# Moving DRAM-to-DRAM copies of an expert table between the stages of a transformer kernel

## What is computed

```python
for i in range(2):                                   # two layers
    kv = mem_n @ mem_w_kv[i]
    x = x + 0.5 * swiglu(rmsnorm(x, norm_g[i, 0]), ffn_w_up[i, 0], ffn_w_down[i, 0])
    x = x + (pool_layer, diff_layer)[i](rmsnorm(x, norm_g[i, 1]), ...)
    x = x + 0.5 * swiglu(rmsnorm(x, norm_g[i, 2]), ffn_w_up[i, 1], ffn_w_down[i, 1])
...
x = x + g1 * hybrid_mixer(h, w_in, w_out, rel_bias)  # the last attention
# experts: 8 heads pick 16 of 16384 each, per token
s = einsum('bthpd,hpnd->bthpn', q, sub_keys); ...; e_idx = ...; g = softmax(g_s)
u = u_emb[e_idx]                                     # rows of U, 16384 x 1024
act = gelu(einsum('btd,bthkd->bthk', h, u))
out = einsum('bthk,bthkd->btd', g * act, v_emb[e_idx])   # rows of V, 16384 x 1024
```

## Time and profile before

| | |
|---|---|
| median of 3 runs | 2007.17 us (2002.93 to 2011.62) |
| profiled execution | 2008.95 us, span 2007.4 us |
| mean granted clock of TensorE | 0.952 |
| PE, DVE, ACT, POOL busy | 1774.0, 1277.5, 795.6, 652.1 us |
| DMA: SP's queue q1 | 346.15 MB, 50.4% of 16 engines' span |
| DMA: POOL's queue q0 | 301.52 MB, 37.6% |

### The profile page before, as it was taken

One profiled execution on the slowest core, in us unless ns is written; L12 is line 12 of the kernel. 1 busy time (PEld: TensorE's weight loads), 2 busy tenths in 40 slices (PEclk: granted clock), 3 DMA queues, 4 the chain that ended last, 5 costly groups with the idle time before them and its releaser, 6 DMA issues.

```text
span 2007.4 us, 22993 instructions
## 1 busy us (share of the span) xinstructions
PE 1774.0 (88%) x8110; PEld 1306.8 (65%) x8110; DVE 1277.5 (64%) x2212; ACT 795.6 (40%) x1423; POOL 652.1 (32%) x602
## 2 busy tenths in 40 slices
PE   7999999999999999999999789788688877778776
PEld 6887898887888779978777788675333333333332
DVE  4566766655466546766655577478999885555554
ACT  5444435544354436665443356432323322211111
POOL 4443560234015440111445112023334433333330
PEclk9999999999999999999999799889889989899998
DMA  8999976799899989758998656368999999999995
GB/s 268 326 373 381 305 257 252 261 348 373 290 313 347 373 282 337 259 206 306 330 335 300 201 193 204 105 256 328 420 420 420 420 420 419 420 421 421 421 421 224
DMA packets 247274, 649.99 MB, mean 324 GB/s; under 512 B 14945, under 2 KB 156562, under 8 KB 214418
## 3 DMA queue, kind: packets, MB, share of 16 engines
q1 hardware_dynamic: 200210, 346.15, 50.4%
q0 software_dynamic: 46304, 301.52, 37.6%
q10 hardware_dynamic: 672, 1.18, 0.3%
HBM read 643.56 MB, written 139.48 MB: 390 GB/s over the span
## 4 chain that ended last, share of the span: by engine, by line
PE 39%; DMA 28%; DVE 16%; POOL 8%; ACT 4%; issue 4%; SPq 0%; ACTq 0%; DVEq 0%; POOLq 0%
DMA late_uv<-uv_rows,M 12%; DMA adaW<-in_w_ada 10%; PE P L1254 6%; PE P L717 3%; PE P L718 3%; PE P L719 3%; PE PX L800 3%; DVE WL L1773 3%; DMA early_uv<-uv_rows,M 3%; PE PX L802 3%; PE PX L801 3%; POOL adaW L554 2%; POOL adaW L555 2%; DVE early_uv L2357 2%; PE P L666 2%
## 5 line engine op out<-in xcount | busy, mean ns | idle before, releaser
L1773 DVE TENSOR_TENSOR WL<-WR,WH 128x1024 fp32r<-128x1024 f32 (+1 forms) x246 | 323.5, 1356 | 213.3 <-ACT WH L1300 213.0
L1300 ACT ACTIVATE WH<-WR 128x1024 fp32r<-128x1024 f32 (+1 forms) x272 | 270.7, 1044 | 357.1 <-PE P L719 154.0
L1254 PE MATMUL P<-early_uv,M 128*128 128x512 f32 x544 | 260.4, 635 | 56.2 <-ACT M L1711 56.2
L1254 PE MATMUL P<-late_uv,M 128*128 128x512 f32 x480 | 240.8, 660 | 78.0 <-ACT M L1711 78.0
L800 PE MATMUL PX<-WH,hTh 128*128 128x512 f32 x704 | 280.8, 399 | 7.6 <-DVE WL L1781 4.3
L802 PE MATMUL PX<-WH,hTl 128*128 128x512 f32 x704 | 275.9, 392 | 0.0
L801 PE MATMUL PX<-WL,hTh 128*128 128x512 f32 x704 | 275.0, 391 | 0.0
L1788 DVE TENSOR_TENSOR WL<-WR,WH 128x1024 fp32r<-128x1024 f32 x128 | 185.1, 1486 | 135.8 <-ACT WH L1309 135.7
L1254 PEld LDWEIGHTS P<-late_uv,M 128*128 128x128 f32 x480 | 99.4, 213 | 218.2 <-issue 117.7
L1254 PEld LDWEIGHTS P<-early_uv,M 128*128 128x128 f32 x544 | 108.0, 203 | 204.5 <-issue 133.6
L651 POOL DMA_INDIRECT early_uv<-uv_rows,M x136 | 130.1, 956 | 286.2 <-PE P L1254 182.9
(11 more groups left out here) (365 smaller groups left out, 3175.7 us busy)
## 6 DMA issues: line engine op xcount, KB each, us to landing
WR<-in_ffn_w_up SPq DMA_DIRECT2D x88, 1024.0 KB, 9.9
WR<-in_ffn_w_down SPq DMA_DIRECT2D x44, 1024.0 KB, 11.1
uv_rows<-in_peer_u SPq DMA_DIRECT2D x35, 1024.0 KB, 13.5
uv_rows<-in_peer_v SPq DMA_DIRECT2D x35, 1024.0 KB, 14.9
uv_rows<-in_peer_u SPq DMA_DIRECT2D x58, 512.0 KB, 9.6
uv_rows<-in_peer_v SPq DMA_DIRECT2D x58, 512.0 KB, 9.1
adaW<-in_w_ada POOLq DMA_DIRECT2D x48, 512.0 KB, 8.1
WR<-in_diff_w_in SPq DMA_DIRECT2D x14, 1024.0 KB, 11.6
```

Of the source, the lines that this page charges most:

```text
L1254: last = mm(P[2 * t + q][:], diag[:, n % 2, i], rows_uv(n)[:, i, D + q * 512:D + q * 512 + 512], start=n % GROUPS == 0 and i == 0, stop=n ...
L1300: nc.scalar.activation(split_view(WH, U % 2, kind, part), raw(c % 2, kind, h, part), copy)\
L1773: tt(split_view(WL, U % 2, kind, part), raw(c % 2, kind, h, part), split_view(WH, U % 2, kind, part).bitcast(F32), ALU.subtract)\
```

## The change

Only the tables of the copies change, and one condition around the copy in the loop, since a count may now be 0 there. `COPIES` and `IN_LOOP` are in units. In sum, before and after: kv 4 and 8 units; pool_in to pool_out 7 and 16; diff_in 14 and 28; diff_out 3 and 6; in2 7 and 28; out2 0 and 2; the four down stages 36 and 24; the written-out chunks of the up stages 9 and 0; the loops 48 and 16. A copy is now of up to 512 rows, where it was of up to 256. The number of copies (pairs of DMAs) falls from 93 to 69.

```diff
-    COPIES = dict(kv0=(1, 1), kv1=(1, 1), pool_in=(1, 1, 1), group=(1,), pool_outx=(1,), pool_out=(1, 1), diff_in=(2,) * 7,
-                  diff_out=(1, 1, 1), in2=(1,) * 7, up00=(0, 0, 0), up01=(1, 1, 1), up10=(1, 1, 1), up11=(1, 1, 1),
-                  down00=(2, 1) * 3, down01=(2, 1) * 3, down10=(2, 1) * 3, down11=(2, 1) * 3)
-    IN_LOOP = (1, 2)
+    COPIES = dict(kv0=(2, 2), kv1=(2, 2), pool_in=(3, 3, 3), group=(2,), pool_outx=(1,), pool_out=(2, 2), diff_in=(4,) * 7,
+                  diff_out=(2, 2, 2), in2=(4,) * 7, out2=(2, 0), up00=(0, 0, 0), up01=(0, 0, 0), up10=(0, 0, 0), up11=(0, 0, 0),
+                  down00=(1,) * 6, down01=(1,) * 6, down10=(1,) * 6, down11=(1,) * 6)
+    IN_LOOP = (0, 1)
...
-            copies += 4 * len(IN_LOOP)
+            copies += 4 * sum(n > 0 for n in IN_LOOP)
...
-                    copy_rows(r * (128 * sum(IN_LOOP)) + (loop_from + 128 * sum(IN_LOOP[:j])), 128 * IN_LOOP[j])
+                    if IN_LOOP[j]:
+                        copy_rows(r * (128 * sum(IN_LOOP)) + (loop_from + 128 * sum(IN_LOOP[:j])), 128 * IN_LOOP[j])
```

## The result

The changed kernel takes 2037.3 us (median of three executions, 2033.7 to 2044.8) against 2005.7 for the kernel before, measured beside it. A fourth execution took 2255.6 us at a mean granted clock of 0.744, a slower state, and is left out. The ratio is 1.0161, with an interval of 1.0131 to 1.0192, so it is about 32 us slower. Measured once more (e11) it took 2041.1 us, with a ratio of 1.0197 (1.0148 to 1.0245). The forecast was 2033, range 1992 to 2087.

What follows compares the result with a forecast made beforehand. The prediction took PE as the bound, held up by DMA transfers as full in the feed-forward layers; 52 us of attention delays less 26 us gained is +26 us, forecast 2033 us, range 1992 to 2087.

Steps and rivals of the forecast that it cites:

- (a): Feed-forward layers: removing 53 of 93 copy units shortens PE's waits and restores its clock, a gain of 26 us.
- upper bound of 31.3 us: Feed-forward layers: the most that could be gained, 24.6 us of PE's waits plus 6.7 us of lost clock.
- adaW step: Feed-forward layers: PE's four waits for the sums of adaW vanish as POOL's transfers speed up, 10.6 us gained.
- (b): Attention stages: added copies make weights land late in SP's queue, delays of 9 + 30 + 13 = 52 us.
- queue sums: Attention stages: copies and weights between two splits take 87.3 us (kv and pool), 139.2 (differential) and 139.2 (last attention).
- cushion: Attention stages: each delay is reduced once by some 3 us lying between a weight split and PE's need of it.
- 3.5 us a unit: Copies of four units: average price, the first two units at 3.0 us, the last two halfway between 3.0 and 4.9.
- (c): SP's issues, POOL's first gather and the expert stage: moved or unchanged at no cost, the gather shifting with the delay.
- 1: Large copies stay slow at 4.9 us a unit, total 2136 us; halfway, at 4.2, 2087; chance 0.15.
- rival 2: Large copies cost 3.0 us a unit: 23 us late against 26 gained, net -3, 2004 us; chance 0.25.
- 3: Units cost 2.6 us as in a short burst, so the attention delays are small: net -20, 1987 us; chance 0.15.
- Rival 4: Expert stage: the last copy ends after 1320 us and sets the start of the gathers; given no chance of its own.

Runs made afterwards that it cites:

- e11: The changed kernel measured once more, unaltered, on another chip against the kernel before; 2041.1 us, ratio 1.0197.
- e1: Against the kernel before: the change's lighter copies in the feed-forward layers only, attention stages as before, 53 units left out; 1978.8 us, ratio 0.9877.
- e8: Against the kernel before: only the up stages' copies lightened as in the change, down and attention stages as before, 41 units left out; 1979.3 us.
- e5: Against the changed kernel: all 128 units spread so that each chunk gets only as many as it has room for; 1979.4 us, ratio 0.9883.
- e12: Changed kernel with the same copies issued in DMAs of 128 rows, a repeat on another chip; 2022.6 us, ratio 1.0097.
- e6: The evenly spread 128 units of e5, with every copy issued in DMAs of 128 rows; 1977.4 us, ratio 0.9853.
- e2: Against the changed kernel: attention stages' copies kept, feed-forward layers' copies as before the change, 53 units copied once more into unread rows; 2040.4 us.
- e13: Changed kernel with the tensor of copied rows allocated with 23168 rows, the first 16384 used; 2044.9 us, ratio 1.0187.

## Why the prediction was right, and which terms were off

**The bound.** The diagnosis held: the layers were crowded, the attention stages nearly full, and the move emptied the one by overfilling the other. The sign, the place of the loss and its order by stage (differential, last attention, pool) came out as forecast.

**(a) The gain, 26 us.** 24.6 us (17 to 32) by e1's ratio, 29 by its PE marks, 30 by those of the changed kernel. So the upper bound of 31.3 us, summed from waits and clock of PE, held; only the sums between splits (33 and 38) pass it, and they count weights that land earlier as a gain. That the adaW step comes from the up stages' load is borne out by e8, with the waits for actL and the clock moving along. POOL's idle time per transfer fell from 7.2 to 5.2 us (247.8 / 48), forecast about 5.

**(b) The delays, 52 us.** Measured 65 between splits and 60 by PE's marks. The queue sums themselves were close:

| queue | predicted, us | measured (split to split) | late before the cushion, predicted | late, measured at splits | late with the cushion, predicted | late, measured by PE's marks |
|---|---|---|---|---|---|---|
| kv and pool | 87.3 | 88.0 | 11.8 | 12.5 | 9 | 8.0 |
| differential | 139.2 | 136.7 | 32.7 | 30.3 | 30 | 30.2 |
| last attention | 139.2 | 145.5 | 16.0 | 22.4 | 13 | 21.9 |

The table shows two terms that were off. The first is the **cushion**. I took 3 us off each delay for the lead of a split over PE's need of it, 9 us in all. Of that 5.0 us were seen (65.1 less 60.1), and nearly all of it in the pool stage; in the differential stage there was none and in the last attention 0.5. PE's waits show a reason that fits: in the differential stage it waits 11.2 us for the attention heads' steps on ACT and DVE and 2.3 for a split. The heads stand behind the late split in ACT's order, so the lead of the split over PE was no protection for them. That is read from one profile and was not tested alone. The 11.5 us a chunk from which I took the cushion, and the full queue, were also read from one pair of issues in the first half of the stage; its seven chunks take 106.5 / 7 = 15.2 us each, and in the kernel before SP's last issue of a chunk in this stage takes 1.0 us. So the queue had room at the end of the stage, which e5 uses.

The second and larger term is one that I left out of the queue of the **last attention stage**, 6.3 us too short. From 1139.95, the split of its second chunk, to 1241.88 lie 5 chunks and 20 units: 101.9 - 30.0 = 71.9, 3.6 us a unit, where the differential stage has (861.38 - 765.11 - 30.0) / 20 = 3.31. That is not a dearer copy. The rate is the same, 331 and 329 GB/s; more bytes pass. SP's queue and POOL's moved from 1140 to 1242 (packets, MB, share)

```profile
q1 hardware_dynamic: 15834, 32.09, 98.9%
q0 software_dynamic: 640, 1.57, 4.5%
```

and from 765 to 861 us there is SP's alone:

```profile
q1 hardware_dynamic: 15699, 31.54, 103.7%
```

2.1 MB more at 331 GB/s are 6.4 us, against 5.7 between the two stretches. POOL's part are its loads of `rel_rows` for this attention, 1.97 MB or some 6 us over the whole stage, before the change as after it. I had counted POOL's transfers in the pool queue and not in this one.

The first four units of a stage were dearer than the rest, 3.98 us in the differential stage. In the last attention (1139.95 - 1114.95 - 6.0) / 4 = 4.75 is no price: this split waits for PE, and in the kernel before, with one unit there, it came nearly as late, 24.4 us after the first.

```profile
1139.95 2.01 ACT L1301 ACTIVATE WH<-WR 128x1024 fp32r<-128x1024 f32 x2 [4.70 <-PE P L669]
```

So the forecast's 3.5 us a unit was about right as a mean ((136.7 - 41.2) / 28 = 3.4 over the differential stage). The guess behind it, that a long copy unbroken by other transfers is slow, fits the first four units but not e12, whose copies are as unbroken and cost 3.26 and 3.08.

Both sides of the sum were forecast too small, the gain at 26 against 30 us and the delays at 52 against 60, and the two errors nearly cancel: +28 in the profile against +26. That the total came so close is luck; that the delays outweigh the gain about two to one is not.

**(c)** held: the gather's wait is unchanged, and the last segment moved by 1.3 us (-1.4 by PE's marks).

**Rivals.** 1 (4.2 to 4.9 us a unit) was approached only by the first four units of the differential stage, at 3.98. 2 and 3 needed 3.0 and 2.6; in the changed kernel neither of the two long stages was that cheap. e12 came near rival 2 in the differential stage, where it loses 21.1 us and rival 2 had 18.7 before the cushion. In the last attention stage it loses 13.4 us where rival 2 had 2: its units cost about 3.1 there too, and POOL's transfers and the wait of the second split for PE are in no rival's sum. Rival 4 did not occur.

**What I had asked the profile to show.** The share of 0.75 to 0.85 was right for the up and later down stages (0.76, 0.84) and too low for the first (0.88). Clock 1.00 and no adaS wait: right. Seven waits of ACT for differential weights: right. PE at 75% was too low (83% in 742 to 865 us), and the last attention stage is late from its third chunk on, not its fourth.

## What to carry to other kernels

Work that shared a queue with weights was free in a stage of this kernel until the queue's time for it passed the engine's time; beyond that every us was paid nearly in full, so spread it up to that line everywhere rather than move it from the fullest stage to the next (e5 and e6 gained 1.2 to 1.5% with the copies that cost the change 1.6%). Sum the queue over the whole stage from its first landing, with what other queues move in it, and don't subtract a lead that other work of the same engine stands behind. Measure a stage at the engine that bounds it as well as at the landings. A second queue did not protect the weights: look at what share of the engines each queue gets.

## What the runs showed of the hardware that I had not expected

- A full queue of weights and copies from DRAM to DRAM moved 325 to 331 GB/s with copies in 512-row DMAs (2 MB), 347 to 355 with 128-row DMAs (0.5 MB). A unit cost 3.98 us at the start of the differential stage and 3.31 behind it, against 3.26 and 3.08.
- Two queues with work share the engines unevenly: 20.8 MB of copies in 5234 packets (4 KB each) against 9.8 MB of weights in 9705 packets (1 KB each), 70.6 and 31.7% of the engines' time.
- With its queue full, SP's issue of a chunk took 13.5 to 14 us at the start of the differential stage, while ACT's issue of a 2 MB copy on a queue of its own took 0.5 us.
- The same 512-row copies ran at 346 GB/s in e2. The allocation alone does not explain it (e13: 331 and 325), and its cause is open.
